# The seats of the tokens in the experts' rounds, from eight products on TensorE instead of a table in memory

## The reference, cut to what matters

```python
g_sel = jnp.argmax(p_g, axis=-1)                       # one group of 4
le = take_along_axis(le, g_sel)                        # its 8 experts
top_p, top_i = lax.top_k(jax.nn.softmax(le, axis=-1), TOP_K)      # 2 of them
experts = (g_sel[:, None] * EXPERTS_PER_GROUP + top_i)
...
hid = jax.nn.silu(xblk @ w_gate[e]) * (xblk @ w_up[e])            # rows of the tokens of expert e
return hid @ w_down[e]
...
y = segment_sum(yb * row_w[:, None], row_tok)          # each token sums its two experts
```

## Time and profile before

| | us |
|---|---|
| median of 3 runs | 2318.07 |
| lowest, highest | 2316.73, 2320.39 |
| profiled execution, its own time | 2321.49 |
| its span in the trace | 2319.8 |
| PE busy | 2080.0 (90%) |
| DVE, ACT, POOL busy | 904.7, 664.5, 363.3 |

### The profile page before, as it was taken

One profiled execution on the slowest core, in us unless ns is written; L12 is line 12 of the kernel. 1 busy time (PEld: TensorE's weight loads), 2 busy tenths in 40 slices (PEclk: granted clock), 3 DMA queues, 4 the chain that ended last, 5 costly groups with the idle time before them and its releaser, 6 DMA issues.

```text
span 2319.8 us, 25950 instructions
## 1 busy us (share of the span) xinstructions
PE 2080.0 (90%) x10252; PEld 1544.2 (67%) x10252; DVE 904.7 (39%) x1162; ACT 664.5 (29%) x840; POOL 363.3 (16%) x354
## 2 busy tenths in 40 slices
PE   6996828877777778999989999999999999999999
PEld 5894713322223227888867888887789987888887
DVE  5535250000000005677765432334775434333332
ACT  3433120000000004666644221223222323221222
POOL 0000020000000001554531110111343101100100
PEclk9997968999999999999989999999999999999999
DMA  5220247999999993121112222223222322222220
GB/s 203 78 105 0 86 181 305 421 422 421 421 421 421 421 410 154 55 73 55 55 62 91 91 95 104 91 90 109 91 74 98 140 73 91 91 91 98 96 97 37
DMA packets 57640, 378.10 MB, mean 163 GB/s; under 512 B 8944, under 2 KB 9040, under 8 KB 13904
## 3 DMA queue, kind: packets, MB, share of 16 engines
q1 hardware_dynamic: 51120, 363.02, 40.0%
q0 software_dynamic: 6432, 13.83, 1.7%
HBM read 370.99 MB, written 15.26 MB: 167 GB/s over the span
## 4 chain that ended last, share of the span: by engine, by line
PE 65%; DMA 18%; DVE 7%; issue 5%; ACT 3%; POOL 1%; SPq 0%; DVEq 0%; POOLq 0%; ACTq 0%
PE bank L556 18%; PE bank L557 18%; PE bank L558 18%; DMA moe_w<-weights_in 17%; PE bank L779 3%; PE bank L756 2%; DVE o_tmp L2185 1%; PE bank L853 1%; DVE k_dec L2161 1%; PE bank L675 1%; PE bank L1176 1%; POOL k_rot L2574 1%; PE bank L954 1%; PE bank L966 1%; DVE ws L2170 0%
## 5 line engine op out<-in xcount | busy, mean ns | idle before, releaser
L556 PE MATMUL bank<-u_hi,w_hi 128*128 128x512 f32 x1152 | 463.3, 402 | 0.7 <-issue 0.7
L557 PE MATMUL bank<-u_lo,w_hi 128*128 128x512 f32 x1152 | 455.5, 395 | 0.0
L558 PE MATMUL bank<-u_hi,w_lo 128*128 128x512 f32 x1152 | 455.1, 395 | 0.0
L1702 DVE TENSOR_TENSOR w_lo<-raw,w_hi 128x2048 fp32r<-128x2048 f32 x96 | 233.1, 2428 | 299.9 <-ACT w_hi L1227 299.7
L756 PE MATMUL bank<-moe_w,xe 128*64 128x512 f32 x1088 | 262.2, 629 | 88.9 <-DMA moe_w<-weights_in 87.7
L756 PEld LDWEIGHTS bank<-moe_w,xe 128*64 128x64 f32 x1088 | 91.1, 144 | 259.1 <-issue 259.0
L1227 ACT ACTIVATE w_hi<-raw 128x2048 fp32r<-128x2048 f32 x96 | 183.7, 1913 | 273.2 <-PE bank L558 272.3
L556 PEld LDWEIGHTS bank<-u_hi,w_hi 128*128 128x128 f32 x1152 | 216.5, 188 | 54.2 <-issue 3.5
L557 PEld LDWEIGHTS bank<-u_lo,w_hi 128*128 128x128 f32 x1152 | 216.5, 188 | 52.6 <-issue 2.4
L558 PEld LDWEIGHTS bank<-u_hi,w_lo 128*128 128x128 f32 x1152 | 216.2, 188 | 53.0
L556 PE MATMUL bank<-w_hi,u_hi 128*128 128x256 f32 (+1 forms) x640 | 191.5, 299 | 7.3 <-issue 7.3
(11 more groups left out here) (415 smaller groups left out, 2756.3 us busy)
## 6 DMA issues: line engine op xcount, KB each, us to landing
moe_w<-weights_in SPq DMA_DIRECT2D x204, 1024.0 KB, 25.2
raw<-weights_in SPq DMA_DIRECT2D x128, 1024.0 KB, 4.8
y_pairs<-pair_rows SPq DMA_DIRECT2D x4, 1024.0 KB, 7.7
res<-x_in SPq DMA_DIRECT2D x1, 2048.0 KB, 7.8
token_rows<-xn POOLq DMA_DIRECT2D x1, 2048.0 KB, 7.0
v_rows<-vals SPq DMA_DIRECT2D x2, 1024.0 KB, 5.7
vals<-v_rows SPq DMA_DIRECT2D x2, 1024.0 KB, 6.8
out<-out_tile SPq DMA_DIRECT2D x4, 512.0 KB, 2.6
```

Source lines behind the costliest of these rows:

```text
L556: nc.tensor.matmul(out_ap, a_hi, b_hi, start=first, stop=False)
L557: nc.tensor.matmul(out_ap, a_hi, b_lo, start=False, stop=False)
L558: return nc.tensor.matmul(out_ap, a_lo, b_hi, start=False, stop=last)
L1702: nc.vector.tensor_tensor(w_lo[:, n % 2], raw[:, n % RAW], w_hi[:, n % 2].bitcast(F32), ALU.subtract) \
```

## The change

The seats of the 16 rounds are no longer read from the table. DVE makes for each token and each of its two experts a row of 128 zeros and ones, `hot`, with the one at its seat (`before` plus 64 for the odd expert of a pair, and pushed beyond 127 if the count is over CAP). It also makes `valued`, [2, TB, 2, 16]: in the column of the token's round, its pair of numbers less 4096, else zero. Eight products on PE, each with `hot` as the loaded operand and 32 columns of `valued` streamed, sum over tokens in bank 7; each seat gets its one token's value, and an empty seat zero. DVE adds 4096.25 and casts to integers into `slots`. POOL then gathers for rounds 0 and 1, and only after that waits for `dest` and fills the table. The table is read back for the extra round and the overflow alone. PE no longer waits for `dest_ready` before it turns the first rows. New tiles lie in space that is free at that time; three old semaphores are used again.

```diff
--- before.py
+++ after.py
@@ -76,8 +76,8 @@
-C_COLS, C_N = columns(("ident", P), ("ones", P), ("upper", P), ("strict", P), ("blocks64", P), ("negmask", P),
-                      ("sel", H1 * P), ("eps", 1), ("iota32", NE), ("lane", NE))
+C_COLS, C_N = columns(("ident", P), ("ones", P), ("upper", P), ("strict", P), ("iota128", P), ("negmask", P),
+                      ("sel", H1 * P), ("eps", 1), ("iota32", NE), ("lane", NE), ("half", NE))
...
@@ -200,6 +200,11 @@
+        hot = place("hot", [2, TB, P], at_b + 14 * KB2)
+        valued = place("valued", [2, TB, 2, NPAIR], at_b + 19 * KB2)
+        pair_hot = place("pair_hot", [2, TB, NPAIR], at_b + 19 * KB2 + 1024)
+        slots_f = place("slots_f", [2, NPAIR], at_b + 19 * KB2 + 1536)
+        taken = place("taken", [2, TB, NE], at_b + 25 * KB2 + 1024)
...
+        below = tiny("below", [TB, 2, 2])
...
@@ -426,6 +432,9 @@
+        hot_ready, HOT_READY = s_weighted, 3 * H1
+        seated, SEATED = s_ready, H1
+        slots_ready, SLOTS_READY = dec_arg, 4 * H1
...
@@ -733,6 +742,12 @@
             everyone = both[:].rearrange("p b e -> p (b e)")
             nc.tensor.matmul(bank[5][:, 0:TB * NE], cols(con, C_COLS, "strict"), everyone, start=True, stop=True)
             nc.tensor.matmul(bank[5][:, TB * NE:2 * TB * NE], ones, everyone, start=True, stop=True).then_inc(before_ready, 1)
+            for k in range(2):
+                pe.wait_ge(hot_ready, HOT_READY + k + 1)
+                for b in range(TB):
+                    mm = nc.tensor.matmul(bank[7][:, 0:2 * NPAIR], hot[:, k, b], valued[:, k, b].rearrange("p c q -> p (c q)"),
+                                          start=k == 0 and b == 0, stop=k == 1 and b == TB - 1)
+            mm.then_inc(seated, 1)
...
@@ -781,7 +796,6 @@
-            pe.wait_ge(dest_ready, 1)
             pe.wait_ge(x_gathered[0], 16)
             turn_rows(0)
...
@@ -1934,6 +1948,8 @@
             chain(nc.vector.tensor_copy(pairs[:], cols(par2, P2_COLS, "pairs").rearrange("p (b k c) -> p b k c", b=TB, k=2)))
+            nc.vector.tensor_scalar(below[:], cols(par2, P2_COLS, "pairs").rearrange("p (b k c) -> p b k c", b=TB, k=2),
+                                    float(-NO_PAIR), None, ALU.add)
             dve.wait_ge(logits_ready, 2)
...
@@ -1955,6 +1971,14 @@
             nc.vector.tensor_tensor(both[:], owns[:, 0], owns[:, 1], ALU.add).then_inc(owns_ready, 1)
 
+            for k in range(2):
+                last = nc.vector.tensor_reduce(pair_hot[:, k], owns[:, k].rearrange("p b (q i) -> p b q i", i=2), AX.X, ALU.add)
+            chain(last)
+            for k in range(2):
+                for c in range(2):
+                    nc.vector.tensor_tensor(valued[:, k, :, c], pair_hot[:, k],
+                                            below[:, :, k, c].unsqueeze(2).to_broadcast([P, TB, NPAIR]), ALU.mult)
+
             dve.wait_ge(router_exp, 1)
             chain(nc.vector.tensor_reduce(best[:, 1], gap[:], AX.X, ALU.add))
...
@@ -1973,13 +1997,27 @@
             before, count = before_all[:], so_far[:, TB - 1]
 
+            nc.vector.tensor_scalar(over[:], before, float(CAP), None, ALU.is_ge)
+            chain(nc.vector.tensor_tensor(row[:], before, cols(con, C_COLS, "half").unsqueeze(1).to_broadcast([P, TB, NE]), ALU.add))
+            chain(nc.vector.scalar_tensor_tensor(row[:], over[:], float(2 * P), row[:], ALU.mult, ALU.add))
+            chain(nc.vector.tensor_tensor(taken[:], owns[:], row[:].unsqueeze(1).to_broadcast([P, 2, TB, NE]), ALU.mult))
+            for k in range(2):
+                last = nc.vector.tensor_reduce(dest_f[:, k], taken[:, k], AX.X, ALU.add)
+            chain(last)
+            for k in range(2):
+                nc.vector.tensor_tensor(hot[:, k], cols(con, C_COLS, "iota128").unsqueeze(1).to_broadcast([P, TB, P]),
+                                        dest_f[:, k].unsqueeze(2).to_broadcast([P, TB, P]), ALU.is_equal).then_inc(hot_ready, 1)
+            dve.wait_ge(seated, SEATED + 1)
+            chain(nc.vector.tensor_scalar(slots_f[:], bank[7][:, 0:2 * NPAIR].rearrange("p (c q) -> p c q", c=2),
+                                          NO_PAIR + 0.25, None, ALU.add))
+            nc.vector.tensor_copy(slots[:, 0:NPAIR], slots_f[:].rearrange("p c q -> p q c")).then_inc(slots_ready, 1)
+
             chain(nc.vector.tensor_scalar(n_over[:], count, 1.0, -0.5 - CAP / 2, ALU.max, ALU.add))
...
             chain(nc.vector.tensor_scalar(over_start[:], over_start[:], float(CAP), float(MAIN - CAP), ALU.mult, ALU.add))
-            chain(nc.vector.tensor_scalar(over[:], before, float(CAP), None, ALU.is_ge))
             chain(nc.vector.tensor_tensor(lift[:], before, over_start[:].unsqueeze(1).to_broadcast([P, TB, NE]), ALU.add))
...
@@ -2450,6 +2488,18 @@
             nc.gpsimd.memset(x_rows[:], 0.0).then_inc(rows_set, 1)
             pool.wait_ge(rows_set, 2)
             pool.wait_ge(table_written, 16)
+
+            def gather(e):
+
+                nc.gpsimd.indirect_dma_start(
+                    out=x_rows[:, e % 2], out_offset=None, in_=token_rows,
+                    in_offset=bass.IndirectOffsetOnAxis(ap=slots[:, e, 0:1], axis=0),
+                    bounds_check=T - 1, oob_is_err=False).then_inc(x_gathered[e % 2], 16)
+
+            pool.wait_ge(slots_ready, SLOTS_READY + 1)
+            pool.wait_ge(slots_landed, 16)
+            gather(0)
+            gather(1)
             pool.wait_ge(dest_ready, 1)
             for b in range(TB):
                 for k in range(2):
@@ -2457,20 +2507,8 @@
                         out=slot_table, out_offset=bass.IndirectOffsetOnAxis(ap=dest[:, k, b:b + 1], axis=0),
                         in_=pairs[:, b, k], in_offset=None).then_inc(table_written, 16)
             pool.wait_ge(table_written, 16 + 16 * 2 * TB)
-            pool.dma_start(slots[:, 0:NPAIR], slot_table[0:MAIN].rearrange("(s e) c -> s e c", s=P)).then_inc(slots_landed, 16)
             pool.dma_start(slots[:, EXTRA], slot_table[MAIN:MAIN + P]).then_inc(slots_landed, 16)
-            pool.wait_ge(slots_landed, 48)
             pool.dma_start(over_slots[0:CAP], slot_table[MAIN + P:].rearrange("(v s) c -> s v c", s=CAP)).then_inc(slots_landed, 16)
-
...
-            gather(0)
-            gather(1)
             for e in range(ROUNDS):
...
@@ -2480,10 +2518,11 @@
                 if e + 2 < ROUNDS:
                     pool.wait_ge(xe_turned, e + 1)
+                    if e + 2 == EXTRA:
+                        pool.wait_ge(slots_landed, 48)
                     gather(e + 2)
-            pool.wait_ge(slots_landed, 64)
...
@@ -2688,10 +2727,11 @@
-        "ident": s == t, "upper": s <= t, "strict": s < t, "ones": np.ones((P, P)), "blocks64": s // 64 == t // 64,
+        "ident": s == t, "upper": s <= t, "strict": s < t, "ones": np.ones((P, P)), "iota128": np.broadcast_to(t, (P, P)),
...
-        "lane": np.broadcast_to(np.arange(NE) % 2 * (CAP * NPAIR) + np.arange(NE) // 2, (P, NE))})
+        "lane": np.broadcast_to(np.arange(NE) % 2 * (CAP * NPAIR) + np.arange(NE) // 2, (P, NE)),
+        "half": np.broadcast_to(np.arange(NE) % 2 * CAP, (P, NE))})
```

More of the change, by code:

```diff
@@ L2459, in _ @@
             pool.wait_ge(table_written, 16 + 16 * 2 * TB)
-            pool.dma_start(slots[:, 0:NPAIR], slot_table[0:MAIN].rearrange("(s e) c -> s e c", s=P)).then_inc(slots_landed, 16)
             pool.dma_start(slots[:, EXTRA], slot_table[MAIN:MAIN + P]).then_inc(slots_landed, 16)
-            pool.wait_ge(slots_landed, 48)
             pool.dma_start(over_slots[0:CAP], slot_table[MAIN + P:].rearrange("(v s) c -> s v c", s=CAP)).then_inc(slots_landed, 16)
-            def gather(e):
-                nc.gpsimd.indirect_dma_start(
-                    out=x_rows[:, e % 2], out_offset=None, in_=token_rows,
-                    in_offset=bass.IndirectOffsetOnAxis(ap=slots[:, e, 0:1], axis=0),
-                    bounds_check=T - 1, oob_is_err=False).then_inc(x_gathered[e % 2], 16)
-            gather(0)
-            gather(1)
             for e in range(ROUNDS):
```

## The result

The changed kernel takes 2310.11 us (median of 7 runs, 2308.31 to 2312.22), the kernel before 2318.56 in the same comparison: ratio 0.9963, 95% interval 0.9952 to 0.9975, so 8.45 us and 0.37% faster (5.8 to 11.1 us by the interval). I had forecast a gain of 11.9 us, a time of 2306.2, and a range to 2309.8: the sign and the mechanism hold, the size does not. Of the 3.9 us between 2306.2 and 2310.11, 0.5 is the kernel before itself, which took 2318.07 us when I forecast and 2318.56 here.

What follows compares the result with a forecast made beforehand. The weight stream was taken to bound the expert rounds, its start held by round 0. DVE's 7.13 us delay against a 19 us wait moves the copy into `xe` 11.9 us earlier: 2318.07 - 11.9 = 2306.2 us, range 2301.8 to 2309.8.

Steps and rivals of the forecast that it cites:

- (a): DVE behind `both`: six added instructions for pair_hot and valued, 1.25 us, net +0.58 as an old wait for PE hides 0.67.
- (b): DVE from before_all to the rows of zeros and ones (`hot`): added instructions costing 3.08 us.
- (c): DVE waits for PE's eight seat products: sixteen loads 0.23 us apart at half clock, a 3.4 us wait.
- (d): DVE ahead of n_over: slots_f 0.22 us and the cast 0.11 us.
- (e): DVE's old chain from n_over to the copy into `xe`: 10.66 us, reaching the copy at 344.59.
- (f): Round 0's gathered rows: gather starts at 334.89, PE turns rows from 339.0 to 340.95, DVE arrives 3.5 us later.
- The late gather: Rival, chance 0.09: round 0's gather lands in 10.3 us, not 4.0; gain 9.2 us, time 2308.9.
- The clock's rise: PE in round 0: before, full level 4.8 us after the first product, with the first pair of units taking 6.3 us.
- (g): POOL's scatters and table loads, now behind dest, cost nothing; constants grow by 16 KB, 0.04 us at 421 GB/s.
- All later work shifts: Behind the first refill: the stream stays saturated and everything later comes earlier by the same 11.9 us.

Runs made afterwards that it cites:

- the tail moved: The change with share_diag, the lbs group, fg_row and ACT's exponential moved behind the first copy into `xe`; 2306.99 us, ratio 0.9939.
- e10_change_again: The change, unaltered, measured once more beside a copy of the kernel before; 2310.54 us, ratio 0.9964.
- e13_before_moved: The kernel before with only 32 unused columns added to the constants, so tiles behind them move by 128 bytes; 2322.74 us, ratio 1.0011.
- e14_half_in_par2: The change with the 32 columns `half` put into par2's free room, so no tile moves; 2306.69 us, ratio 0.9942.
- e8_before_tail: The kernel before with share_diag, the lbs group, fg_row and ACT's exponential moved behind the first copy into `xe`; 2321.47 us, ratio 1.0013.
- e15_best: The change with the tail moved, over_slots loaded in its branch, seats in reduced f32, and `half` in par2; 2296.4 us, ratio 0.99.
- e3_branch: The change with the load of over_slots moved into the overflow branch, which is not taken with these inputs; 2312.56 us.

## Why the prediction was wrong

- *(a) pair_hot and valued*, net +0.58: +0.40 (so_far 2.07 us behind `both`, before 1.67). The two reductions took 0.47 us together, where I had 0.29 + 0.40.
- *(b)* 3.08: 3.05, from over at 324.92 to the end of hot at 327.97.
- *(c) the wait for eight products*, 3.4: 3.12. Sixteen loads in 3.49 us at a granted clock of 0.50, 0.22 each: the pitch of the loads was the right row. The Trainium skill's price by columns (TensorE: Matmul & The Clock Gate, section LDWEIGHTS), 107 ns each, is off by two here; in the reduced type there are half as many loads, still 0.22 each.
- *(d)* 0.33: 0.32. *(e)* The DVE chain brings the copy 12.4 us earlier; the forecast was 11.9.
- *(f)* PE turned the rows 15.13 us behind `both`; the forecast was 15.4. DVE came 3.4 us later (forecast 3.5); with the tail moved, the 3.4 us came out. The late gather did not happen: 4.19 us from its start to PE, and POOL's instruction took 1.07 us as before, with DVE's small operations beside it. The clock's rise came 4.0 us after the first product, in the rows below, and the first pair took 5.8 us, not 6.3. (For the kernel before I had read the rise as 362.3. A mean of 0.70 from 362 to 363 puts it at 362.6, 5.1 us after the first product.) The changed kernel's clock (us, PE busy, PEclk, DMA share, GB/s):

```profile
344.00:346.00 2.00, 2.00 (x8) 0.50 0.08 9
346.00:348.00 2.00, 2.00 (x8) 0.73 0.03 1
348.00:349.00 1.00, 1.00 (x8) 1.00 0.03 1
```

- *(g) is the step that failed, twice.* It put the scatters and the table's two loads at nothing ("Cost nothing"), with an eye on who waits for them, and nobody does. But they now run inside a stream that has no slack: 0.8 us of it for the load of over_slots alone. The other 0.5 of the 1.3 us was not tested: the scatters' end and the load for the extra round lie there too, but the 180 refills of kernels whose table work ends ahead of the stream also differ by 0.5 among themselves (450.62 to 451.14). And (g) put the constants at "0.04 us at 421 GB/s", the price of moving them, not of shifting what lies behind them: the 128 bytes cost 2.7 us in the dense layers, more than any other error here. "All later work shifts" was thus wrong by 2.7.
- *The sum*: 12.4 + 0.5 (the clock) - 1.3 - 2.7 = 8.9 us, against 8.5, 9.7 and 8.1 measured. The stated range took in runs and clock by 1 us and had no term for either loss; it ended 0.3 us below the result. Two small errors went my way and hid part of the losses: 0.5 in (a) to (c), and the 0.5 of the clock, which is luck. In e10_change_again the same program used its first pair in 6.6 us, and its lead at y_pairs was 11.0.
- *How far the sum is shown.* The two first profiles do not show it by themselves. From y_pairs to the end the change took only 0.5 us more (1438.14 against 1437.65), for three other shared stretches were shorter in that execution by 1.1, 0.8 and 0.5 us. The 2.7 us rest on the dense layers, equal in every profile of a kind, and on two medians: 0.5 to 4.6 us lost by e13_before_moved, and 13.2 gained by e14_half_in_par2. If 2.7 us are charged to every kernel with moved tiles, medians and leads at y_pairs agree within 2.3 us in all but two: e8_before_tail is 3.4 slower than its lead says, e15_best 6.9 faster.

What stays open are these two, and the attention layer between the dense ones. This shared code took 293.4 us in the profiles of the kernel before, its copy and e8_before_tail, and 287.2 to 297.2 in the others, with no order that I can see. It was shortest in e15_best, whose lead at y_pairs explains 16.7 of its 23.5 us; 6.2 us of the rest are this layer in its profile. It was longest in e3_branch. Why a move of 128 bytes slows the matmuls was not tried further.

## What to carry to other kernels

When a long queue is taken off the path, look at what stands in order on the engine that must act next: here 3.4 us of work for later stages had been free only because of the wait. Work put "off the path" beside a saturated DMA stream can be paid in that stream: here 7 KB in 896 pieces cost some forty times what their bytes would. And when a gain arrives only in part, cut both kernels off at the place where the trace shows it in full, and compare shared stages one by one: 32 unused columns in the constants reproduced the loss alone.

## What the runs showed of the hardware

- Moving all tiles behind the constants by 128 bytes lengthened two PE-bound layers at full clock by 0.4% and 0.3% (370.2 to 371.7, 365.0 to 366.2 us), in ten profiles against five. Between the kernel before and e13_before_moved the unused columns are the only edit.
- One load of 896 pieces of 8 bytes, 7 KB, took 0.7 to 0.8 us of a stream of 421 GB/s, in which it would be 0.02 us by its bytes. It landed 7.9 us behind its issue there, and 2.7 where no stream ran.
- The same program got PE's full clock 4.0 us behind its first expert product in one execution and some 5.7 in another, with PE busy throughout from that product on; the first pair of weight buffers took 5.8 and 6.6 us.
